# Two places in a transformer-block pair kernel: when TensorE turns the modulation sums, and when VectorE scales the first block's output

## The reference

```python
def first_block(x, c, w_ada, ...):
    mod = c_act @ w_ada[l] + b_ada[l]                  # 1024 -> 6 * 1024
    sh1, sc1, ga1, sh2, sc2, ga2 = jnp.split(mod, 6, axis=-1)
    x = x + ga1 * (mixed @ w_out[l])                   # after attention
    h2 = rmsnorm(x, g_ffn[l]) * (1.0 + sc2) + sh2
    gate, up = jnp.split(h2 @ w_gu[l], 2, axis=-1)     # 1024 -> 2 * 2816
    x = x + ga2 * ((jax.nn.silu(gate) * up) @ w_down[l])
    return rmsnorm(x, g_final)

def second_block(x, c, norm_g, mod_w, ...):
    shift, scale, gate = jnp.split(c_act @ mod_w[l] + mod_b[l], 3, axis=-1)
    h = rmsnorm_2(x, norm_g[l]) * (1.0 + scale) + shift
    u = h @ w_in[l]                                    # 1024 -> 5 * 1024, in parts cv, cg, cs, lx, ls
    v = causal_depthwise_conv(cv * jax.nn.sigmoid(cg), dw_w[l], dw_b[l])   # 31 taps
    v = jax.nn.silu(layernorm(v, cln_g[l], cln_b[l])) @ pw2_w[l] + pw2_b[l]
    y_conv = v * jax.nn.silu(cs)
    y_lru = ...                                        # recurrent branch, from lx and ls
    y = jnp.concatenate([y_conv, y_lru], axis=-1) @ w_out[l]
    x = x + (1.0 + gate) * y
    return rmsnorm_2(x, final_g)
```

## Time and profile before

| | |
|---|---|
| median of three runs | 1058.49 us (1057.61 to 1058.69) |
| the profiled execution, its own time | 1058.71 us |
| its span (first to last instruction) | 1056.9 us |
| TensorE busy | 1034.2 us, 98% |
| VectorE, GpSimd, ScalarE busy | 668.2, 471.9, 431.8 us |
| mean granted TensorE clock | 0.993 of full |
| load from device memory, mean | 121 GB/s |

### The profile page before, as it was taken

One profiled execution on the slowest core, in us unless ns is written; L12 is line 12 of the kernel. 1 busy time (PEld: TensorE's weight loads), 2 busy tenths in 40 slices (PEclk: granted clock), 3 DMA queues, 4 the chain that ended last, 5 costly groups with the idle time before them and its releaser, 6 DMA issues.

```text
span 1056.9 us, 13979 instructions
## 1 busy us (share of the span) xinstructions
PE 1034.2 (98%) x5166; PEld 834.9 (79%) x5166; DVE 668.2 (63%) x1268; ACT 431.8 (41%) x601; POOL 471.9 (45%) x176
## 2 busy tenths in 40 slices
PE   7999999999999999999999999999999999989997
PEld 5687796667877888888888888888887778878886
DVE  5367997777774332223437223599999999974322
ACT  4244325883361221212232323434526877262232
POOL 0034342692333453443533544356865666633340
PEclk9999999999998999999999999999999999999999
DMA  9994231140415435434364233225231323313312
GB/s 325 349 288 125 78 121 40 42 161 1 146 54 175 143 119 161 157 121 156 119 217 163 85 104 110 80 82 157 80 120 40 95 81 104 99 61 100 99 40 79
DMA packets 127250, 128.90 MB, mean 122 GB/s; under 512 B 3552, under 2 KB 125280, under 8 KB 127200
## 3 DMA queue, kind: packets, MB, share of 16 engines
q1 hardware_dynamic: 125952, 127.38, 37.4%
q10 hardware_dynamic: 1248, 0.86, 0.3%
HBM read 126.13 MB, written 2.10 MB: 121 GB/s over the span
## 4 chain that ended last, share of the span: by engine, by line
PE 87%; DVE 6%; ACT 2%; DMA 1%; SPq 1%; issue 1%; POOL 1%; DVEq 0%; ACTq 0%
PE bank L734 22%; PE bank L736 22%; PE bank L735 22%; PE bank L1079 2%; PE bank L1050 2%; PE bank L922 2%; DVE bank L2308 2%; DMA ada_stage<-in_w_ada 1%; PE bank L1263 1%; PE bank L746 1%; PE bank L748 1%; PE bank L747 1%; POOL w_lo L608 1%; PE bank L940 1%; PE bank L759 1%
## 5 line engine op out<-in xcount | busy, mean ns | idle before, releaser
L608 POOL TENSOR_TENSOR w_lo<-w_stage,w_hi 128x2048 fp32r<-128x2048 f32 x77 | 368.5, 4786 | 488.8 <-ACT w_hi L1376 488.8
L734 PE MATMUL bank<-act_hi,w_hi 128*128 128x512 f32 x832 | 330.1, 397 | 0.1
L736 PE MATMUL bank<-act_hi,w_lo 128*128 128x512 f32 x832 | 324.8, 390 | 0.0
L735 PE MATMUL bank<-act_lo,w_hi 128*128 128x512 f32 x832 | 324.7, 390 | 0.0
L1376 ACT ACTIVATE w_hi<-w_stage 128x2048 fp32r<-128x2048 f32 x78 | 149.3, 1914 | 233.3 <-PE bank L736 218.4
L734 PEld LDWEIGHTS bank<-act_hi,w_hi 128*128 128x128 f32 x832 | 156.9, 189 | 38.0 <-issue 4.9
L735 PEld LDWEIGHTS bank<-act_lo,w_hi 128*128 128x128 f32 x832 | 156.9, 189 | 33.1 <-issue 1.4
L736 PEld LDWEIGHTS bank<-act_hi,w_lo 128*128 128x128 f32 x832 | 156.7, 188 | 32.9
L2308 DVE SCALAR_TENSOR_TENSOR bank<-v_pad,vcol,bank 128x512 f32<-128x512 f32 x208 | 138.2, 746 | 0.0
L2214 DVE TENSOR_TENSOR tmp<-bank,tmp 128x512 f32<-128x512 f32 x22 | 15.1, 690 | 149.1 <-PE bank L736 149.1
L734 PE MATMUL bank<-ff_hi,w_hi 128*128 128x512 f32 x176 | 69.7, 396 | 0.0
(11 more groups left out here) (352 smaller groups left out, 1641.2 us busy)
## 6 DMA issues: line engine op xcount, KB each, us to landing
w_stage<-in_w_in SPq DMA_DIRECT2D x29, 1024.0 KB, 5.2
w_stage<-in_w_gu SPq DMA_DIRECT2D x22, 1024.0 KB, 5.2
ada_stage<-in_w_ada SPq DMA_DIRECT2D x20, 1024.0 KB, 11.4
w_stage<-in_w_out SPq DMA_DIRECT2D x12, 1024.0 KB, 5.1
ada_stage<-in_mod_w SPq DMA_DIRECT2D x12, 1024.0 KB, 7.6
w_stage<-in_w_down SPq DMA_DIRECT2D x8, 1024.0 KB, 5.2
late_stage<-in_w_ada SPq DMA_DIRECT2D x4, 1024.0 KB, 8.5
w_stage<-in_pw_w SPq DMA_DIRECT2D x4, 1024.0 KB, 5.2
```

What stands on the lines that cost most here:

```text
L608: nc.gpsimd.tensor_tensor(w_lo[b][:], w_stage[b][:], w_hi[b][:].bitcast(F32), ALU.subtract).then_inc(s_lo, 1)
L734: pe.matmul(dst, wh, rhs_hi(k), start=(first and k == 0), stop=False)
L735: pe.matmul(dst, wh, rhs_lo(k), start=False, stop=False)
L736: mm = pe.matmul(dst, wl, rhs_hi(k), start=False, stop=(last and k == n_k - 1))
```

## The change

There are two edits, on different engines. On TensorE, `gu_modulations(0)` goes from ahead of the loop into it: the sums of round `j - 1` are turned between the gate tiles and the up tiles of round `j`, and those of the last round behind the loop. On VectorE, the six rows that were scaled in one piece ahead of the centring are spread out: rows 2 and 3 come behind the squares, just ahead of their residuals; rows 4, 5 and 6 stand in the norm's loop one row ahead of their residual, and row 7 behind it. Each residual now waits for its own scaled row.

```diff
             abreast([(bank[2][:], b1, low, s_guacc), (bank[3][:], b1, high, s_wused)], 1)
-            gu_modulations(0)
             with pe.Fori(1, KF // 2) as j:
                 for q in range(2):
                     b = (C_GU + q) % 2
@@ -1199,7 +1198,9 @@
                         pe.wait_ge((s_silu, s_up)[q], j * 2 + (1 + m))
                         tile(bank[2 * q + m][:], b, slice(m * P, (m + 1) * P), KD, hi, lo).then_inc((s_guacc, s_wused)[m], 1)
-                gu_modulations(j)
+                    if q == 0:
+                        gu_modulations(j - 1)
+            gu_modulations(KF // 2 - 1)
@@ -2373,16 +2374,16 @@
                 residual_2(C_LRU, 2 * KD, t)
-            for k in range(MEAN_AFTER + 1, KD):
-                first_block_out(k)
             dve.wait_ge(s_mspread, 1)
             for k in range(KD):
                 V.tensor_tensor(conv[:, k, :], conv[:, k, :], bank[MEAN_BANK][:], ALU.subtract).then_inc(s_cen, 1)
                 if k >= 1:
                     add_squares(k - 1)
             add_squares(KD - 1)
-            dve.wait_ge(s_x1, KD)
             for t in range(MEAN_AFTER + 1, VAR_AFTER + 1):
+                first_block_out(t)
+            for t in range(MEAN_AFTER + 1, VAR_AFTER + 1):
+                dve.wait_ge(s_x1, t + 1)
                 residual_2(C_LRU, 2 * KD, t)
@@ -2397,10 +2398,15 @@
+                if k + 1 in RES_AT:
+                    first_block_out(t)
                 if k in RES_AT:
+                    dve.wait_ge(s_x1, t + 1)
                     residual_2(C_LRU, 2 * KD, t)
                     t += 1
             for t in range(t, KD):
+                first_block_out(t)
+                dve.wait_ge(s_x1, t + 1)
                 residual_2(C_LRU, 2 * KD, t)
```

## The result

The changed kernel takes 1048.09 us, the median of four runs (1047.82 to 1048.30). The kernel before, run beside it, takes 1058.45 us (1057.61 to 1058.69). The ratio is 0.9903, with a 95% interval from 0.9886 to 0.9921: 1% faster. The profiled execution takes 1048.1 us, its span is 1046.3 us (1056.9 before), and the mean granted clock is 0.999 where it was 0.993.

A forecast was written before the change was run, and what follows sets the result against it. TensorE, busy for 98%, was taken to bound the kernel, with two long waits. 1058.71 less 6.34 (modulation sums) less 4.7 (sums of squares) gave 1047.7 us; the forecast's own range was 1046.5 to 1049.5, the wider one 1046.3 to 1052.0.

The forecast's parts named there:

- place 1: TensorE's 3.1 us wait before the modulation sums (line 1186): gain 6.34 us, 3.3 of waiting, the rest slow clock.
- place 2: TensorE's 3.0 us wait before the sums of squares (line 780): centring starts 4.6 us earlier, gain 4.7 us.
- the late sums: Late modulation sums in the down projection: fourth has 1.1 us slack; cost taken as 0, under 1 us if missed.
- The round of 22.21 us: Steady-state round of the gate and up loop: ten such rounds from 315.62 put the last sums at 537.75.
- The loop's entry: Start of the gate and up loop: entering straight from a product costs nothing visible; a later loop showed 0.22 us.
- the back edge: Return of the gate and up loop, formerly beside the sums: no cost taken, 5 us at worst over ten times.
- VectorE's steps fit: Modulation steps in mid-round: end 15.5 us in, before TensorE ends the first up tile at about 16.7.
- rival (c): SyncE's mid-round wait makes weight chunks late, so TensorE waits in each of nine rounds: 1066 us, slower, 3%.
- two megabytes in some 7 us: Second down-projection chunk, loaded beside one more megabyte: lands near 545, ScalarE wants it at 544.3.
- rival (a): Second moved row behind the squares meets GpSimd and is held, so the wait for squares gives nothing: 1053.5 us, 10%.
- The norm's loop: Four scaled rows placed there: one held until 948.1, last low part at about 954.8, 1.9 us left, no cost.

The follow-up runs named there:

- the filled wait: Kernel before, with 15 idle 128 x 128 products put ahead of the first modulation sums so TensorE works through its wait: 1055.85 us, ratio 0.9982.
- Three remedies: Changed kernel, one edit each: second down chunk loaded before SyncE's wait, 1047.68 us; small vector kept in PSUM, 1047.92; fourth late chunk summed one group later, 1047.78.
- the rows alone: Kernel before with only the VectorE edit (scaled rows spread out), the loop's sums in their old order: 1052.93 us, ratio 0.9953.
- the gain in PSUM: Kernel before, order kept, the six scaled rows reading the gain from a PSUM copy instead of SBUF: 1054.26 us, ratio 0.9960.
- the last experiment: Changed kernel with the 128 x 8 vector that line 2242 writes kept in PSUM, ScalarE reading it there: 1047.92 us, ratio 0.9902.

## Why the prediction was right

The forecast was 1047.7 us, the result is 1048.09. Both main steps held, by the mechanism forecast and nearly by its size. In the profiled run, 0.43 us above the forecast, place 1 gave 0.20 us less, place 2 0.06 less, the late sums cost 0.33 that were set to nothing, and 0.08 are in the rest. That line 748 came 0.23 us sooner took part of this off again, by chance.

- **Place 1**, forecast 6.34 us, measured 6.14. The round of 22.21 us held (the last sums were forecast for 537.75 and came at 537.72, but that so small a difference is left is luck: line 748 was 0.23 us early). The loop's entry took 0.29 us instead of the 0.22 that the later loop had shown, and from the loop's first product to the last sums it was 222.27 us, forecast 222.1: no cost at the back edge beyond 0.02 us a round. The split between pause and clock, which was argued, is shown by the trace of the filled wait: 3.25 and 2.89 us, forecast 3.3 and 3.0.
- **VectorE's steps fit** in the middle of the round with 1.49 us to spare, forecast 1.2 (16.7 - 15.5). SyncE's wait in mid-round, rival (c), never decided: the weight load goes out at 334.31, right behind GpSimd's end at 334.12, when the steps have been over for 3 us, and TensorE waits in no round.
- **The late sums** are the term that failed: "1.1 us of slack for a chain that may come up to 0.7 later. I take 0". The chunk was forecast to land 0.7 us after ScalarE wanted it and was 2.3 us late; 1.7 us of this reached the fourth sum. The slack was used up, and the price was 0.33 us, within the "under 1 us" given. (The slack was in truth 1.5 us and not 1.1: the 571.54 of the earlier trace rows is the start of a group that begins with the third sum, and the fourth is wanted about 0.5 us later.) SyncE's start was right (531.11 + 6.4 = 537.5, forecast 537.4). What was left out of "two megabytes in some 7 us" is the third down chunk, which now follows at once, and from 537.92 on the next late chunk: the windows from 532 to 540 moved some 2.6 MB, and 9 us went by from 531.11 to 540.1. Nor did the forecast see how the delay gets to VectorE, through a small instruction that is held until GpSimd ends; it counted such a hold at place 2 and not here, though the trace before had one of 4.38 us. Three remedies, each at another link (the load, the hold, the sum's place), give the loss back. That the other loads' share made the landing late is worked out from the rows; moving the third chunk alone wasn't tried.
- **Place 2**, forecast 4.7 us, measured 4.64. The centring starts at 915.01 (forecast 914.7), after 2.33 us of idling (forecast 2). The second row began at 925.01 and GpSimd at 925.58: this is the half microsecond that the prediction set against rival (a), and it came out at 0.57 us. The row was not held, though its last 0.17 us ran beside GpSimd. The six rows in one piece show what stood on the other side of that margin.
- **The norm's loop**: one row held, as forecast, for 3.41 us (forecast 4, until GpSimd ends), and the last low part with 1.9 us to spare, forecast 1.9. On the held row the Trainium skill ("SBUF — State Buffer", Who interferes with whom) and the runs agree: two operands in SBUF are held (3.41 us and, in the kernel before, 3.75), one operand in PSUM isn't (six in 4.04 us beside the same GpSimd instruction).

## What to carry to other kernels

Both pauses of TensorE were a matter of order and not of work. At place 1 the waiting product stood too early: it went behind products whose inputs were ready. At place 2 VectorE did work that nobody wanted yet ahead of work that TensorE waited for. A new place has to leave slack to the engine that makes the input and to the queue that waits for the same event. One tried a few microseconds off cost the gain: the sums at the end of the round made the kernel slower than before, and the rows in one piece behind the squares left no clear gain. A pause cost more than its length here, 6.1 us for 3.1 at place 1 and 4.6 for 3.0 at place 2, as the slow clock followed both, though not every pause (below). And where VectorE works with two operands in SBUF just ahead of a critical step, one of them should be in PSUM, or GpSimd be idle.

## What the runs showed of the hardware

The time of the kernel before varies more than that of the changed one, and goes with the mean granted clock. Over 19 runs on one chip it lay between 1055.37 us (clock 0.997) and 1060.43 us (0.991), with 14 of them from 1057.0 to 1058.8 (0.996 to 0.993). The changed kernel's eight runs lay between 1047.78 and 1048.55 us, all at 0.998 or 0.999; its variants without a pause between 1047.54 and 1048.07, but for one run (1049.03, at 0.997). So most of the spread is gone with the pauses. With place 1's pause alone (the rows alone) three runs lay between 1052.48 and 1052.93 us at 0.996 to 0.997 and two at 1054.16 and 1054.43 at 0.995. This suggests that the low-clock stretch behind a pause isn't of one length; by the traces it isn't shown, for the three that have this pause (before, the rows alone, the gain in PSUM) agree: 228.70, 228.96 and 228.81 us from line 748 to the last sums. All three are of executions in the slower part of their runs, so the 2.89 us may be near the long end. What sets the length in a given run was not tried.

A pause isn't always followed by a slow stretch: with the sums at the end of the round, a wait of 2.24 us left the clock at 1.00 in its window and the next, while one of 2.34 us stands in a window at 0.68. TensorE's two instructions with what they waited for, then the windows (columns as in the earlier trace rows):

```profile
557.50 0.50 PE L734 MATMUL bank<-ff_hi,w_hi 128*128 128x512 f32 x1 [2.24 <-POOL w_lo L608]
...
576.48 0.71 PE L829 MATMUL bank<-ones,tmp 128*128 128x1 f32 x4 [2.34 <-DVE tmp L1834]
```

```profile
555.00:560.00 5.00, 2.76 (x13) 2.07 (x12) 3.18 (x6) 2.22 (x3) 2.45 (x1) 1.00 0.86 259
560.00:565.00 5.00, 5.00 (x24) 4.10 (x23) 4.72 (x16) 2.87 (x4) 2.01 (x1) 1.00 1.08 360
...
575.00:580.00 5.00, 3.52 (x11) 2.95 (x12) 4.82 (x13) 0.00 (x0) 0.46 (x1) 0.68 0.55 157
```

A very small VectorE instruction is held as long as a large one, each until GpSimd ended: 128 x 8 numbers for 3.09 us, and for 4.38 in the kernel before, 128 x 512 for 3.41. The one of 3.09 us (line 2242) reads one operand from SBUF and writes to SBUF. The Trainium skill ("SBUF — State Buffer", Who interferes with whom) counts this operation among those that can take the pair of ports that GpSimd shares, and the last experiment agrees: written to PSUM it took 0.17 us. The next small one there with two operands in SBUF (line 2246, 128 x 8) was held, from 545.48 to 546.30, and GpSimd ended at 546.28.
